# The three weight sums of each paired tile, computed by GpSimd instead of VectorE

## The reference

```python
hn = _rmsnorm(x, pre_g).astype(x.dtype)
proj = jnp.einsum('bld,de->ble', hn, w_in).astype(F32)   # d = 1024, once per layer
```

## Time and profile before

| | before |
|---|---|
| median of three runs | 2100.09 us |
| the profiled execution, its own time | 2102.05 us |
| its span, first to last instruction | 2100.3 us |
| granted clock of TensorE, mean | 0.983 |
| PE busy | 2028.6 us, 97% |
| DVE busy | 1246.1 us, 59% |
| ACT busy | 792.6 us, 38% |
| POOL busy | 266.8 us, 13% |

### The profile page before, as it was taken

How to read it: one execution, slowest core, us unless ns; L and a number is a source line. 1 busy time by engine, 2 the same in 40 slices (tenths; PEclk the granted TensorE clock), 3 DMA queues, 4 the chain that set the end, 5 groups by cost and what they waited for, 6 DMA issues and landing times. The chain is left out here.

```text
span 2100.3 us, 33193 instructions
## 1 busy us (share of the span) xinstructions
PE 2028.6 (97%) x12862; PEld 1804.5 (86%) x12862; DVE 1246.1 (59%) x2213; ACT 792.6 (38%) x1476; POOL 266.8 (13%) x378
## 2 busy tenths in 40 slices
PE   7999999999999899999969999999999799999997
PEld 7999999999999677787659999999999677777774
DVE  5466676645564666666656557676655465455543
ACT  6555543323231544444335344332212343333323
POOL 0000000000000621111100000000000452323222
PEclk9999999999999899999979999999999899999999
DMA  3121232443333754554342332444334554545442
GB/s 141 56 65 50 66 101 76 150 154 94 113 104 99 236 167 145 169 169 151 93 136 76 94 92 78 135 146 135 110 97 116 180 173 164 183 165 181 162 153 72
DMA packets 210407, 264.92 MB, mean 126 GB/s; under 512 B 49284, under 2 KB 157060, under 8 KB 208216
## 3 DMA queue, kind: packets, MB, share of 16 engines
q1 hardware_dynamic: 210264, 262.95, 39.9%
HBM read 172.91 MB, written 89.99 MB: 125 GB/s over the span
## 5 line engine op out<-in xcount | busy, mean ns | idle before, releaser
L588 DVE TENSOR_TENSOR pa_stage<-pa_ps,pa_stage 128x536 f32<-128x536 f32 x110 | 77.0, 712 | 119.3 <-PE pa_ps L555 111.0
L588 DVE TENSOR_TENSOR pc_stage<-pc_ps,pc_stage 128x536 f32<-128x536 f32 x110 | 77.0, 712 | 97.3 <-PE pc_ps L555 77.6
L402 PE MATMUL pa_ps<-a_XT_hi,pa_w_hi 128*128 128x358 f32 x576 | 133.2, 340 | 0.3 <-PEq L209 0.3
L402 PE MATMUL pa_ps<-a_XT_hi,pa_w_lo 128*128 128x358 f32 x576 | 125.9, 327 | 0.0
L402 PE MATMUL pa_ps<-a_XT_lo,pa_w_hi 128*128 128x358 f32 x576 | 125.8, 326 | 0.0
L1477 PE MATMUL mc_ps<-mc_wout_hi,mc_mix_hi 128*128 128x512 f32 x256 | 105.9, 414 | 5.0 <-POOL mc_mix_lo L3193 5.0
L555 PE MATMUL pc_ps<-c_XT_hi,pc_w_hi 128*128 128x268 f32 x384 | 110.2, 287 | 0.0
L555 PE MATMUL pa_ps<-a_XT_hi,pa_w_lo 128*128 128x268 f32 x384 | 110.1, 287 | 0.0
L555 PE MATMUL pc_ps<-c_XT_hi,pc_w_lo 128*128 128x268 f32 x384 | 110.1, 287 | 0.0
L555 PE MATMUL pc_ps<-c_XT_lo,pc_w_hi 128*128 128x268 f32 x384 | 110.1, 287 | 0.0
L555 PE MATMUL pa_ps<-a_XT_lo,pa_w_hi 128*128 128x268 f32 x384 | 110.0, 287 | 0.0
(11 more groups left out here) (576 smaller groups left out, 5948.2 us busy)
## 6 DMA issues: line engine op xcount, KB each, us to landing
pa_w_raw<-in_w_a SPq DMA_DIRECT2D x57, 512.0 KB, 4.6
pc_w_raw<-in_w_c SPq DMA_DIRECT2D x49, 512.0 KB, 4.6
scr_c<-pc_stage SPq DMA_DIRECT2D x48, 512.0 KB, 3.2
scr_a<-pa_stage SPq DMA_DIRECT2D x40, 512.0 KB, 3.2
mc_sample_state<-in_s SPq DMA_DIRECT2D x32, 512.0 KB, 4.6
out_s_s<-mc_sample_state SPq DMA_DIRECT2D x32, 512.0 KB, 2.8
ma_sample_state<-in_c SPq DMA_DIRECT2D x32, 257.0 KB, 4.1
out_c_s<-ma_sample_state SPq DMA_DIRECT2D x32, 257.0 KB, 3.0
```

The lines of the kernel that those rows point to most:

```text
L402: ins = pe.matmul(self.ps[:, 3 * s + t, 0:TC], w[:, k, :], x[:, k, t * TC:(t + 1) * TC], start=(k == 0 and j == 0), stop=(k == KT - 1 and ...
L588: dve.tensor_tensor(dst, self.out(p, product), x, ALU.add).then_inc(self.added, 1)
```

## The change

`sum_weights` takes POOL as its engine. The calls are taken out of DVE's order, and POOL gets a loop of its own in each projection, which makes the sums of one pair after another, as soon as both raw tiles are in and the sums before have been split. In stage A a wait stands ahead of the loop until the RG-LRU rows, in whose room the sums lie, have been stored. The four instructions, their operands, their waits and the signals they give are the same.

```diff
-    def sum_weights(self, dve, p):
+    def sum_weights(self, pool, p):
         for s in range(2):
-            dve.wait_ge(self.loaded[s], 16 * p + 16)
+            pool.wait_ge(self.loaded[s], 16 * p + 16)
...
-        dve.tensor_tensor(s[:, 0, :, :], low[:, 0:KH, :], low[:, KH:KT, :], ALU.add).then_inc(self.chain, 1)
+        pool.tensor_tensor(s[:, 0, :, :], low[:, 0:KH, :], low[:, KH:KT, :], ALU.add).then_inc(self.chain, 1)
...
             self.add(dve, p, 3, upper[1], lower[1], 3)
-            if more:
-                self.sum_weights(dve, p + 1)
             self.add(dve, p, 7, lower[1], lower[1], 4)
...
-                HP.sum_weights(dve, 0)
                 HP.t3_sum(dve, 0)
...
+                pool.wait_ge(lru_spilled, 32 * 8)
+                for p in range(NPAIR):
+                    HP.sum_weights(pool, p)
...
                     HP.t_sums(dve, i)
-                    if i == 7:
-                        HP.sum_weights(dve, 0)
                     dve.wait_ge(soft_ready, i + 1)
...
+            @block.gpsimd
+            def _(pool):
+                for p in range(NPAIR):
+                    HP.sum_weights(pool, p)
```

More of the change, by code:

```diff
@@ L473, in load @@
         sp.dma_start(self.G.raw[s][:], self.G.w_d[self.tiles[p] + s]).then_inc(self.loaded[s], 16)
-    def sum_weights(self, dve, p):
+    def sum_weights(self, pool, p):
         for s in range(2):
-            dve.wait_ge(self.loaded[s], 16 * p + 16)
+            pool.wait_ge(self.loaded[s], 16 * p + 16)
         if p:
-            dve.wait_ge(self.sums_ready, p)
+            pool.wait_ge(self.sums_ready, p)
         up, low = self.G.raw
         s = self.sums
-        dve.tensor_tensor(s[:, 0, :, :], low[:, 0:KH, :], low[:, KH:KT, :], ALU.add).then_inc(self.chain, 1)
[L484 to L488, removed]
+        pool.tensor_tensor(s[:, 0, :, :], low[:, 0:KH, :], low[:, KH:KT, :], ALU.add).then_inc(self.chain, 1)
+        pool.wait_ge(self.chain, 2 * p + 1)
+        pool.tensor_tensor(s[:, 1, :, :], s[:, 0, :, :], up[:, 0:KH, :], ALU.subtract).then_inc(self.chain, 1)
+        pool.tensor_tensor(low[:, 0:KH, :], up[:, 0:KH, :], low[:, 0:KH, :], ALU.subtract)
+        pool.wait_ge(self.chain, 2 * p + 2)
+        pool.tensor_tensor(s[:, 2, :, :], up[:, KH:KT, :], s[:, 1, :, :], ALU.subtract).then_inc(self.summed, 1)
     def split_upper_hi(self, act, p):
```

## The result

Over 20 executions of each kernel on the same chip, the changed kernel takes 2108.38 us in the median and the kernel before 2102.60. The ratio is 1.0025, with a 95% interval of 1.0018 to 1.0031: 5.3 us slower (3.8 to 6.5). One execution of the changed kernel, of 9157.08 us, is left out of the ratio. The profiled execution of the changed kernel happens to be a short one (2104.34, span 2102.5); other stages vary by as much as the change costs, so the places are compared by PE's waits, not by the spans.

The account below looks back on a forecast made before the run. PE, busy in every microsecond of the pairs, was taken as the bound. Terms 0 + 1.3 (stage A, pair 1) + 2.1 (stage C, pair 0) = +3.4 us on the median 2100.09 gave 2103.5, range 2097 to 2109.

Parts of the forecast that it names:

- the caught t3_sum: Stage C, pair 0: POOL's second batch lands among t3_sum's last three instructions, +3.6 us more, 2107.1; chance 0.10.
- What bounds it: In the pairs PE is always busy, so the 87.6 us leaving DVE gain nothing; at most 0.9 us to win.
- Stage A, pair 0, zero: Low halves have 3.4 us of cover before PE's use; DVE at most 2.4 us later, so zero cost.
- Stage A, pair 1, +1.3: The tight place: POOL's sums, taking turns with DVE's L500, end late and PE waits; +1.3 us, bounds +0.65 and +1.8.
- Stage C, pair 0, +2.1: Softplus, scan and centring take turns with POOL, so PE's wait for product 5's copy grows 2.1 us; bounds -0.6 to +2.1.
- Pairs from 2 on, zero in both stages: POOL's sums end at about 412.0 to 413.2 in pair 2, under 7 us of cover: zero cost.
- POOL could end as late as 420.0: Pair 2: PE's use at 423.26 less ACT's split (1.49) and DVE's low half (1.76); the cover of under 7 us.
- No turn for the scan: Rival: the scan, or anything, takes no turn with POOL; sum 0 to +1.3 us, 2100.1 to 2101.4; chance 0.25.
- Slower in every pair: Rival: POOL instructions above 3.3 us, each further microsecond of four costing 28 us over both stages; 0.06 including something unseen.
- Faster: Rival: DVE's freed 87.6 us reach PE, a gain of over 6.3 us, 2093.8 or less; chance 0.04.

Follow-up runs that it names:

- the runs with more work: Stage A's sums on POOL, C's on DVE, two, three or four extra subtractions in pairs 2-15: 1.0084, 1.0162, 1.0235; only C's pairs 9-15, four extra: 1.0067.
- two extra: Changed kernel with stage C's sums back on DVE and two more POOL subtractions in each of A's pairs 2 to 15: 2119.41 us, ratio 1.0084.
- the kernel with all three mended: Changed kernel with A's pair 1 load earlier, C's gate sigmoid before the split, C's pair 0 sums on DVE: 2101.57 us, ratio 0.9998.
- four subtractions: Changed kernel with stage C's sums back on DVE and four more POOL subtractions in each of A's pairs 2 to 15: 2154.24 us, ratio 1.0235.

## Why the prediction was right, and where it was not

The forecast was 2103.5 us (+3.4), no change by more than 0.3%; measured is +5.3 (+0.25%). The time of 2108.38 lies 0.6 below the upper end of the range, and 2.5 of what lies between it and 2103.5 is the kernel before itself, 2102.60 over 20 executions where the first three had 2100.09. That the range reached so far is luck: its upper end came from the caught t3_sum, which did not happen.

- *What bounds it: right.* The sums' 87.6 us left DVE, its busy time fell from 1246.1 to 1181.9 us, and no wait of PE went with it.
- *Stage A, pair 0, zero: right.* POOL's four took 1.61 to 1.77 each beside DVE, and PE has no wait there.
- *Stage A, pair 1, +1.3: right in size, by a turn, though the other way round.* PE's wait went from 0.27 to 1.65, +1.4. I let POOL go first and L500 wait; L500 went first, lost nothing, and POOL's first waited. POOL ended at 379.64, in the 379.3 to 379.8 worked out. (The lower of these values is 379.3 - 378.12 = 1.2 late, not 1.3.) With the same work this wait was 1.4 to 2.1 in the other kernels.
- *Stage C, pair 0, +2.1: the turns are there, the scan's too, but the term was 0.6 too large; measured +1.5 (against 0.62; in the other kernels with pair 0's sums on DVE the wait was 0.2 to 0.5).* The softplus came as drawn: it ended at 1289.43 + 4.00 = 1293.43, in the prediction at 1293.5. Behind it I counted 1.3 us or more for each turn, the length of a POOL instruction. DVE lost less in the trace: 0.97 in the scan, 0.89 and 1.04 in the two small instructions, 2.90 together, where the prediction's times come to 2.1 + 1.35 = 3.45. POOL's second ended 1.13 after the softplus, its third 1.07 after the scan. The prediction named the Trainium skill's rule on page "SBUF — State Buffer", section "Who interferes with whom", that a DVE instruction with two SBUF inputs contends with a GpSimd instruction that reads SBUF. The scan's 3.36 against 2.39 us agrees with it.
- *Pairs from 2 on, zero in both stages: no wait in A, wrong in C, measured +2.0.* This is the step that failed. "POOL could end as late as 420.0" followed the sums forward to PE's next use of them, and nowhere else. ACT, DVE and SP work in order, and behind the sums stand the finishing of the tile, its store and the next load. Along that ring, by estimates from the runs with more work, a plain pair (one whose finishing has no DVE product) can hide some 2.4 us more of POOL's work in A (two extra, 2.67 us, made 21.1 of 20.82) and 3.3 in C. In C's gated pairs the 1.04 us by which the sums end later were already more than the 0.86 that there was, or the 0.45 on average (20.82 - 20.37). A's four z pairs had no room to speak of either: 23.8 less 2.67 is 21.1, and in the changed kernel their loads come every 20.96 us (549.90 to 612.78). PE does not wait in these few pairs, but no 7 us of cover stand behind it.
- *The rivals.* No turn for the scan: refuted. t3_sum caught: not here; its last instruction started at 1314.81, and POOL's second batch at 1316.89. Slower in every pair: the price that I gave needed 3.3 us per POOL instruction; by the estimates above a plain pair starts to pay at 0.6 to 0.8 more for each of the four (2.4 / 4, 3.3 / 4), so near 1.9 to 2.1. Faster: refuted by the kernel with all three mended, where DVE is freed in 31 of 32 batches and the ratio is 0.9998 (0.9988 to 1.0007).

The two errors, 0.6 too much and 2.0 too little, partly cancel, which is luck too: they make 1.4, so PE's waits come to +4.8. The last 0.5 of the measured 5.3 is within its interval.

## What to carry to other kernels

Cover is not the time to the next use of a result. Follow the moved work round to itself, through every in-order engine and queue, to the load of its own next inputs, and compare that ring with the bound engine's time per round: a ring at 19.96 of 20.82 has 0.86 us to give, however late the result is used. Where the helper and the engine that it relieves both read two tiles from SBUF, charge a turn to every such neighbour, the smallest too, and look for a place where the two are not both busy.

## What the runs showed of the hardware

A DVE subtraction on 128 x 8 elements, 0.18 us alone, takes 1.07 beside a POOL subtraction of 128 x 512, and POOL's takes up to 3.36 where it takes 1.29 alone: what has to wait waits for the other's instruction to end, whatever its own size. DVE's additions out of PSUM took no turn: the one at 374.52 in the changed kernel took 0.71 us beside POOL, as it did before. TensorE's granted clock stayed at 1.00, the upper level of 2.4 GHz, through a stretch of 50 us in which PE waited 5.3 us in steps of up to 1.9, and had a mean of 0.90 where it waited as long in steps of up to 3.2, and of 0.88 with 8.6 us in steps of up to 4.4. What in the waits decides was not tried. With four subtractions PE's waits were 32 us and the kernel was 49 slower: a ring that is too long can lose more than it shows as waiting.
